# Turning the attention probabilities by 32 x 32 blocks and weighing them 512 weight columns later, with every block carried from SBUF to SBUF by the weights' queue

## The chip, the cores and the metric

The kernel runs on one core of a Trainium2 chip. The metric is device time in microseconds (us), the median of several executions; profiles come from one execution each. PE is TensorE, ACT is ScalarE, DVE is VectorE, POOL is GpSimd, SP is SyncE, which here only issues transfers.

## The reference, cut to what matters

One layer of a bidirectional encoder on 256 tokens with 2048 channels: RMS norm, one wide projection, a state-space branch and an attention branch, both projected up and merged by gates, an output projection, and an MLP of four times the width. The part that the change touches is attention (16 query heads in 4 groups, 4 key/value heads of 128):

```python
q = rms_norm(q.reshape(b, s, 16, 128), q_norm_g); k = rms_norm(k.reshape(b, s, 4, 128), k_norm_g)
q = apply_rope(q, cos, sin); k = apply_rope(k, cos, sin)
sc = jnp.einsum('blkrd,bskd->bkrls', qblk * d ** -0.5, k).astype(jnp.float32)
prob = jax.nn.softmax(sc, axis=-1).astype(v.dtype)
y_attn = jnp.einsum('bkrls,bskd->blkrd', prob, v)
...
merged = jax.nn.sigmoid(gate_a) * (y_ssm @ w_ssm_up) + jax.nn.sigmoid(gate_b) * (y_attn @ w_attn_up)
x = x + merged @ w_out
```

All is float32. The kernel splits each operand of a large product into a high part (rounded by a copy) and a low part (what is left), and multiplies high by high, high by low and low by high.

## The kernel before

The weights are read once, in windows of 2048 rows by 512 columns. A window is 8 pieces of 512 KB, and a piece of w_ssm_up, w_attn_up or w_out is 12 matmuls of 512 columns on PE (`three_passes`, L1835 to L1837). The function `walk` lists the windows, and with each one the work that is done beside it ("sides"); every engine runs through the same list, so the order of its instructions follows from it: for each piece p, first the weights' own work, then each side's function with that p, in the order of the list. For a piece, SP issues the load into one of four raw buffers (L641) once VectorE has split the piece four before it (`lo_made`); ScalarE makes the high part whi three pieces ahead of PE (L668), as soon as PE is done with the piece four before it (`used`); VectorE makes the low part wlo two pieces ahead in its list (L1108).

A **block round** turns a 256 x 512 part (tokens x channels) into channels x tokens without PE: VectorE transposes each 32 x 32 block in place (`turn_blocks`, L1146), ScalarE's queue writes all of it to DRAM (`put_blocks`, L691, 512 KB), and later reads it back with the blocks in their new places (`get_blocks`, L701, four transfers of 128 KB). There are 15 such rounds: four of z, five of rope's heads (k, then four groups of q), three of merged, three of the residual.

**Attention** runs in four windows, ssm_up 0 to 3, called the first to fourth attention window here. The side `attend` of group g has four heads h. PE makes the scores of head p at pieces p = 0 to 3 (six matmuls of 256 columns into PSUM bank S[h % 2]). VectorE takes the largest (mx, L1487) and scales it (nb, L1490); ScalarE makes the exponentials and their sums (prob, L957); VectorE multiplies by the reciprocal (rden L1494, prob L1497). Then at pieces 3 to 6 PE turns the probabilities of a head with four transposes (`turn`, L1990), ScalarE and VectorE split the turned tile (pT_hi L965, pT_lo L1502), and at pieces 4 to 7 PE weighs the values with them (`weigh`, six matmuls on pT and vg into S[:, 3]). Every second head, at pieces 5 and 7, ScalarE and VectorE take the result into the attention output (a_both, L970 and L1509; a_hi and a_lo below). Beside the first attention window, rope's last group of heads (`rope`, VectorE L1449 to L1472 with two steps on GpSimd, and a turning) and the fetch of the third (`heads_in`, L941 on ScalarE, L1481 on VectorE) are done; beside the second the fetch of the last and the first gating (`gated_a`, L1529).

## Time and profile before

| | |
|---|---|
| median of 3 runs | 1610.12 us (1608.63 to 1610.78) |
| profiled execution | 1609.39 us, span 1607.3 us |
| PE busy | 1595.4 us, 99% of the span |
| PE weight loads | 1349.2 us, 84% |
| VectorE busy | 1278.8 us, 80% |
| ScalarE busy | 928.0 us, 58% |
| transfers of the weights' queue (q1) | 302.2 MB, 58.5% of 16 engines' span |
| transfers of ScalarE's queue (q10) | 24.4 MB, 5.2% |
| granted clock of PE | 0.998 of full |

The profile is of one execution. Busy times of PE are those of pipelined matmuls: a matmul of 512 columns is shown as 0.39 us long, and the next starts 0.23 us after it. So time on PE is read from starts, not from durations. A wait is shown as the idle time before an instruction with the engine that ended it.

### The profile page before, as it was taken

Reading aid. Unit: us, or ns where it says so; the run is one execution under the profiler, and the core shown is the slowest. Engines: PE = TensorE matmul, PEld = TensorE weight load, DVE = VectorE, ACT = ScalarE, POOL = GpSimd, SP = SyncE. Lnnn points to the kernel's source line nnn. Section 1 sums busy time; section 2 is a strip of 40 time slices with the busy share of each in tenths; the row PEclk is TensorE's granted clock in tenths of the full one; section 3 lists DMA queues with packets and bytes.
Section 4 is the critical chain, followed back from the end, with each engine's and each line's share of the span. In section 5 each row is a group of like instructions: output and inputs, shape, how many; then the busy total and the mean of one; then the engine's idle time right before and its main releaser. Section 6 shows DMA issues by size and latency. Waiting matters only on the chain.

```text
span 1607.3 us, 20614 instructions
## 1 busy us (share of the span) xinstructions
PE 1595.4 (99%) x7984; PEld 1349.2 (84%) x7984; DVE 1278.8 (80%) x1521; ACT 928.0 (58%) x1264; POOL 79.2 (5%) x67
## 2 busy tenths in 40 slices
PE   9999999999999999999999999999999999999998
PEld 7888888888888888888888888888888888888886
DVE  7978877888767688876666667999899988998893
ACT  7665566665666545554445555665566655655562
POOL 3000000000000134000000000000000000000000
PEclk9999999999999999999999999999999999999999
DMA  7665656665688776545877875558645863686461
GB/s 272 202 201 184 201 183 211 197 198 185 196 244 238 231 225 200 172 145 181 244 265 235 278 228 178 181 171 266 188 133 200 275 192 123 204 281 214 143 244 53
DMA packets 144993, 327.93 MB, mean 204 GB/s; under 512 B 10944, under 2 KB 19328, under 8 KB 144768
## 3 DMA queue, kind: packets, MB, share of 16 engines
q1 hardware_dynamic: 129376, 302.21, 58.5%
q10 hardware_dynamic: 15520, 24.41, 5.2%
q8 instruction: 63, 1.03, 0.2%
q14 instruction: 34, 0.28, 0.1%
HBM read 316.55 MB, written 10.03 MB: 203 GB/s over the span
## 4 chain that ended last, share of the span: by engine, by line
PE 95%; DVE 2%; issue 1%; DMA 1%; ACT 0%; POOL 0%; POOLq 0%; SPq 0%; ACTq 0%
PE G L1835 17%; PE G L1836 17%; PE G L1837 17%; PE G L1844 13%; PE S L1844 7%; PE G L1848 6%; PE S L1835 4%; PE S L1836 4%; PE S L1837 4%; PE S L1848 4%; PE S L1962 1%; DMA raw<-in_w_in 1%; DVE wlo L1108 1%; PE S L1990 0%; PE S L1939 0%
## 5 line engine op out<-in xcount | busy, mean ns | idle before, releaser
L668 ACT ACTIVATE whi<-raw 128x1024 fp32r<-128x1024 f32 x395 | 416.6, 1059 | 396.4 <-PE G L1837 230.4
L1108 DVE TENSOR_TENSOR wlo<-raw,whi 128x1024 fp32r<-128x1024 f32 x395 | 483.3, 1238 | 132.1 <-ACT whi L668 130.5
L1835 PE MATMUL G<-whi,a_both 128*128 128x512 f32 x768 | 300.0, 391 | 2.5 <-DVE wlo L1108 2.0
L1837 PE MATMUL G<-whi,a_both 128*128 128x512 f32 x768 | 299.0, 389 | 0.0
L1836 PE MATMUL G<-wlo,a_both 128*128 128x512 f32 x768 | 299.0, 389 | 0.0
L1844 PE MATMUL G<-a_both,whi 128*128 128x512 f32 x640 | 201.5, 396 | 0.0
L1835 PEld LDWEIGHTS G<-whi,a_both 128*128 128x128 f32 x768 | 144.2, 188 | 34.0 <-issue 2.8
L1837 PEld LDWEIGHTS G<-whi,a_both 128*128 128x128 f32 x768 | 144.2, 188 | 30.2
L1836 PEld LDWEIGHTS G<-wlo,a_both 128*128 128x128 f32 x768 | 144.2, 188 | 28.9
L1848 PEld LDWEIGHTS G<-a_both,wlo 128*128 128x128 f32 x640 | 120.2, 188 | 28.3
L1835 PE MATMUL G<-whi,b_hi 128*128 128x512 f32 x342 | 133.5, 390 | 0.0
L1836 PE MATMUL G<-wlo,b_hi 128*128 128x512 f32 x342 | 133.4, 390 | 0.0
L1837 PE MATMUL G<-whi,b_lo 128*128 128x512 f32 x342 | 133.1, 389 | 0.0
L668 ACT ACTIVATE whi_late<-raw 128x1024 fp32r<-128x1024 f32 x85 | 89.0, 1058 | 66.2 <-PE S L1848 22.3
L1848 PE MATMUL G<-a_both,wlo 128*128 128x256 f32 x640 | 125.8, 278 | 0.0
L1108 DVE TENSOR_TENSOR wlo_late<-raw,whi_late 128x1024 fp32r<-128x1024 f32 x85 | 102.4, 1221 | 24.1 <-ACT whi_late L668 23.8
L668 ACT ACTIVATE whi_late<-gates 128x1024 fp32r<-128x1024 f32 x67 | 70.1, 1057 | 49.2 <-PE G L1848 18.3
L1844 PEld LDWEIGHTS G<-a_both,whi 128*128 128x128 f32 x640 | 97.5, 189 | 0.1
L1108 DVE TENSOR_TENSOR wlo_late<-gates,whi_late 128x1024 fp32r<-128x1024 f32 x67 | 81.1, 1221 | 18.5 <-ACT whi_late L668 18.5
L668 ACT ACTIVATE whi<-gates 128x1024 fp32r<-128x1024 f32 x63 | 66.1, 1055 | 38.1 <-PE G L1848 13.9
L1108 DVE TENSOR_TENSOR wlo<-gates,whi 128x1024 fp32r<-128x1024 f32 x63 | 76.4, 1221 | 12.7 <-ACT whi L668 12.1
L1844 PE MATMUL G<-a_both,whi_late 128*128 128x512 f32 x256 | 80.5, 396 | 0.0
(313 smaller groups left out, 2689.1 us busy)
## 6 DMA issues: line engine op xcount, KB each, us to landing
raw<-in_w_in SPq DMA_DIRECT2D x208, 512.0 KB, 4.4
raw<-in_w_mlp_in SPq DMA_DIRECT2D x74, 512.0 KB, 4.6
raw<-in_w_mlp_out SPq DMA_DIRECT2D x74, 512.0 KB, 4.9
gates<-in_w_mlp_in SPq DMA_DIRECT2D x54, 512.0 KB, 4.2
gates<-in_w_mlp_out SPq DMA_DIRECT2D x54, 512.0 KB, 4.8
raw<-in_w_ssm_up SPq DMA_DIRECT2D x32, 512.0 KB, 3.8
raw<-in_w_attn_up SPq DMA_DIRECT2D x32, 512.0 KB, 4.5
raw<-in_w_out SPq DMA_DIRECT2D x32, 512.0 KB, 5.2
```

The costliest lines, as they stand in the source:

```text
L668: act.activation(high(m), piece(n), ACT.Copy).then_inc(hi_made, 1)
L1108: dve.tensor_tensor(low(m), piece(n), high(m).bitcast(F32), ALU.subtract).then_inc(lo_made, 1)
L1835: pe.matmul(out_ap, hi[:, k, cols], w_hi, start=start, stop=False)
L1836: pe.matmul(out_ap, hi[:, k, cols], w_lo, start=False, stop=False)
L1837: return pe.matmul(out_ap, lo[:, k, cols], w_hi, start=False, stop=stop)
L1844: pe.matmul(banks[:, c, :], high(m)[:, cols[kk]], a_both[:, 2 * p + kk, :, :].rearrange("p h t -> p (h t)"), start=(p + kk == 0), stop=False)
L1848: last = pe.matmul(banks[:, c, 0:T], low(m)[:, cols[kk]], a_hi[:, 2 * p + kk, :], start=False, stop=(2 * p + kk == KT - 1))
L1962: last = pe.matmul(S[:, 2, (4 * c + h) * HD:(4 * c + h + 1) * HD], mw[:, 0, h, c, :], tm[:, c, h * HD:(h + 1) * HD], start=True, stop=True)
```

## The change

Three things change. First, the blocks of all rounds go from SBUF to SBUF: for each of the 16 pairs (i, j) one transfer of 32 partitions by 256 numbers, 32 KB (`block_across`). SP issues them between the loads of the weights, four after a load, seven pieces behind the load just issued (`SP_LAG`). `put_blocks`, `get_blocks` and the DRAM tensor are gone. Second, the probabilities take the same way, two heads at a time: VectorE turns their blocks (`turn_prob`, two transposes of 128x512), 16 transfers carry them, and ScalarE and VectorE split 1024 columns at once; PE's transposes and bank S[:, 2] for them are gone. Third, everything behind that moves to a new side, `weighed`, one window later: the weighing of heads 0 and 1 stands at piece 3, of heads 2 and 3 at piece 5. In the first attention window `rope` stands ahead of `attend`. A few buffers lie elsewhere. The pieces of the diff stand in the order of the kernel: constants and helpers, the order table, SP's loads, ScalarE, VectorE, PE.

```diff
-    window(13, 0, "ssm_up", 0, [("heads_in", 3), ("attend", 0), ("rope", 4)])
-    window(13, 1, "ssm_up", 1, [("heads_in", 4), ("attend", 1), ("gated_a", 0)])
-    window(14, 0, "ssm_up", 2, [("attend", 2), ("gated_a", 1)])
-    window(14, 1, "ssm_up", 3, [("attend", 3), ("gated_a", 2)])
-    window(15, 0, "attn_up", 0, [("gated_a", 3)])
+    window(13, 0, "ssm_up", 0, [("heads_in", 3), ("rope", 4), ("attend", 0)])
+    window(13, 1, "ssm_up", 1, [("weighed", 0), ("heads_in", 4), ("attend", 1), ("gated_a", 0)])
+    window(14, 0, "ssm_up", 2, [("weighed", 1), ("attend", 2), ("gated_a", 1)])
+    window(14, 1, "ssm_up", 3, [("weighed", 2), ("attend", 3), ("gated_a", 2)])
+    window(15, 0, "attn_up", 0, [("weighed", 3), ("gated_a", 3)])
...
+SP_LAG = 7
...
+        def block_across(i, j, src, dst):
+            return sp.dma_start(dst[Q * j:Q * (j + 1), i, :, :, :].rearrange("p c b t -> p (c b t)"),
+                                src[Q * i:Q * (i + 1), j, :, :, :].rearrange("p c b t -> p (c b t)"))
+
+        def across(rnd, j, src, dst):
+
+            d = BLOCK_ROUNDS.index(rnd)
+            sp.wait_ge(blocks_turned, d + 1)
+            for i in range(4):
+                block_across(i, j, src, dst).then_inc(s_across, 16)
+
+        def rope(p, n):
+            if p == 6 and n:
+                sp.wait_ge(r_lo, n)
+            if p >= 6:
+                across(("rope", n), p - 6, rope_blocks(n), last_heads if n == 4 else head_blocks)
...
+        def pair_across(g, pair, b0, b1):
+
+            sp.wait_ge(at_turned, 2 * g + pair + 1)
+            if g:
+                sp.wait_ge(at_pt_lo, 2 * g - 1 + pair)
+            elif pair:
+                sp.wait_ge(r_lo, 4)
+            for b in range(b0, b1):
+                block_across(b % 4, b // 4, prob_blocks[pair], prob_in[pair]).then_inc(at_across[pair], 16)
+
+        def attend(p, g):
+            if p in (3, 4):
+                pair_across(g, 0, 6 * (p - 3), 6 * (p - 3) + 6)
+            if p == 5:
+                pair_across(g, 0, 12, 16)
+            if p in (6, 7):
+                pair_across(g, 1, 6 * (p - 6), 6 * (p - 6) + 6)
+
+        def weighed(p, g):
+            if p == 0:
+                pair_across(g, 1, 12, 16)
...
                 sp.dma_start(dst, src).then_inc(landed[piece_slot(n)], 16)
+                if n >= SP_LAG:
+                    then, done_beside = BESIDE[n - SP_LAG]
+                    for name, at in done_beside:
+                        if name in table:
+                            table[name](then, at)
...
-            def copy_pt(h):
-                act.wait_ge(at_t, 4 * g + h + 1)
-                if 4 * g + h:
-                    act.wait_ge(at_pv, 4 * g + h)
-                act.activation(pT_hi[:, :, :].rearrange("p s l -> p (s l)"), S[:, 2, :], ACT.Copy
-                               ).then_inc(at_pt, 1)
+            if p < 4:
+                exps(p)
+
+        def weighed(p, g, pr, pp):
+            def high_pt(pair):
+                act.wait_ge(at_across[pair], 256 * (g + 1))
+                if 2 * g + pair:
+                    act.wait_ge(at_pv, 4 * g + 2 * pair)
+                act.activation(by_block(pT_hi, 0, 4), prob_wide[pair], ACT.Copy).then_inc(at_pt, 1)
...
-            if 3 <= p < 7:
-                copy_pt(p - 3)
+            if p == 1:
+                high_pt(0)
+            if p == 3:
+                high(0)
+            if p == 4:
+                high_pt(1)
             if p == 5:
-                high(0)
-            if p < 4:
-                exps(p)
-            if p == 7:
                 high(1)
...
-            def low_pt(h):
-                dve.wait_ge(at_pt, 4 * g + h + 1)
-                dve.tensor_tensor(pT_lo[:, :, :].rearrange("p s l -> p (s l)"), S[:, 2, :],
-                                  pT_hi[:, :, :].rearrange("p s l -> p (s l)").bitcast(F32), ALU.subtract
-                                  ).then_inc(at_pt_lo, 1)
+            def turn_prob(pair):
+                dve.wait_ge(at_v, (4 * g + 2 * pair + 2) * AT_V)
+                if g:
+                    dve.wait_ge(at_across[pair], 256 * g)
+                elif pair:
+                    dve.wait_ge(r_v, 5 * ROPE_V)
+                for tb in range(TB):
+                    last = dve.transpose(
+                        prob_blocks[pair][:, :, :, tb, :].rearrange("p j c t -> p c j t"),
+                        prob[:, tb, 2 * pair:2 * pair + 2, :].rearrange("p h (s j w) -> p (h s) j w", s=TB, w=Q))
+                last.then_inc(at_turned, 1)
+
+            if p < 4:
+                biggest(p)
+            if 1 <= p < 5:
+                normalise(p - 1)
+            if p == 3:
+                turn_prob(0)
+            if p == 5:
+                turn_prob(1)
+
+        def weighed(p, g, pr, pp):
+            def low_pt(pair):
+                dve.wait_ge(at_pt, 2 * g + pair + 1)
+                dve.tensor_tensor(by_block(pT_lo, 0, 4), prob_wide[pair], by_block(pT_hi, 0, 4).bitcast(F32),
+                                  ALU.subtract).then_inc(at_pt_lo, 1)
...
-            if p < 4:
-                biggest(p)
-            if 3 <= p < 7:
-                low_pt(p - 3)
-            if 1 <= p < 5:
-                normalise(p - 1)
+            if p == 1:
+                low_pt(0)
+            if p == 3:
+                low(0)
+            if p == 4:
+                low_pt(1)
             if p == 5:
-                low(0)
-            if p == 7:
                 low(1)
...
-                if h >= 2:
+                if g or h >= 2:
                     pe.wait_ge(at_exp, 8 * g + 2 * (h - 1))
...
-            def turn(h):
-                pe.wait_ge(at_v, (4 * g + h + 1) * AT_V)
-                if 4 * g + h:
-                    pe.wait_ge(at_pt_lo, 4 * g + h)
-                for sb in range(TB):
-                    for tb in range(TB):
-                        last = pe.transpose(S[:, 2, sb * T + tb * P:sb * T + (tb + 1) * P],
-                                            prob[:, h, tb, sb * P:(sb + 1) * P], ident[:, :])
-                last.then_inc(at_t, 1)
-
+            if p < 4:
+                scores(p)
+
+        def weighed(p, g, pr, pp):
             def weigh(h):
-                pe.wait_ge(at_pt_lo, 4 * g + h + 1)
+                pe.wait_ge(at_pt_lo, 2 * g + h // 2 + 1)
...
-            if 3 <= p < 7:
-                turn(p - 3)
-            if p < 4:
-                scores(p)
-            if 4 <= p < 8:
-                weigh(p - 4)
+            if p == 3:
+                weigh(0)
+                weigh(1)
+            if p == 5:
+                weigh(2)
+                weigh(3)
```

On PE, the weighing of head 2 in the first attention window, ahead of the next piece of the weights (G is the weights' product, S the attention's banks). Before:

```order
L1837 MATMUL G<-whi,b_lo 128x512
L1990 MATMUL S<-ident,prob 128x128 x4
L1835 MATMUL S<-pT_hi,vg_hi 128x256
L1836 MATMUL S<-pT_lo,vg_hi 128x256
L1837 MATMUL S<-pT_hi,vg_lo 128x256
```

After, at piece 3 of the second attention window, the first of the twelve matmuls that weigh group 0's heads 0 and 1:

```order
L1926 MATMUL G<-whi,b_lo 128x512
L1924 MATMUL S<-pT_hi,vg_hi 128x256
L1925 MATMUL S<-pT_lo,vg_hi 128x256
L1926 MATMUL S<-pT_hi,vg_lo 128x256
```

The transposes are gone, and two heads are weighed in one go.

On VectorE, pieces 3 and 4 of the second attention window (wlo is the weights' low part, mx to prob belong to the scores of group 1). Before:

```order
L1108 TENSOR_TENSOR wlo<-raw,whi 128x1024 [waits hi_made]
L1487 TENSOR_REDUCE mx<-S 128x2 [waits at_sc]
L1490 TENSOR_SCALAR nb<-mx 128x2 [waits at_max]
L1502 TENSOR_TENSOR pT_lo<-S,pT_hi 128x512 [waits at_pt]
L1494 RECIPROCAL rden<-den 128x2 [waits at_exp]
L1497 TENSOR_SCALAR prob<-prob,rden 128x256 [waits at_v]
L1497 TENSOR_SCALAR prob<-prob,rden 128x256
L1108 TENSOR_TENSOR wlo<-raw,whi 128x1024 [waits hi_made]
L1502 TENSOR_TENSOR pT_lo<-S,pT_hi 128x512 [waits at_pt]
```

After (the numbers at the buffers' ends are the compiler's):

```order
L1178 TENSOR_TENSOR wlo<-raw,whi 128x1024 [waits hi_made]
L1600 TENSOR_TENSOR a_both<-S,a_both 128x2x256 [waits at_hi]
L1557 TENSOR_REDUCE mx<-S 128x2 [waits at_sc]
L1560 TENSOR_SCALAR nb<-mx 128x2 [waits at_max]
L1564 RECIPROCAL rden<-den 128x2 [waits at_exp]
L1567 TENSOR_SCALAR prob<-prob,rden 128x256 [waits at_v]
L1567 TENSOR_SCALAR prob<-prob,rden 128x256
L1577 STREAM_TRANSPOSE prob_blocks_126<-prob 128x4x4x32 [waits at_across0,at_v]
L1577 STREAM_TRANSPOSE prob_blocks_126<-prob 128x4x4x32
L1178 TENSOR_TENSOR wlo<-raw,whi 128x1024 [waits hi_made]
L1594 TENSOR_TENSOR pT_lo<-head_blocks,pT_hi 128x1024 [waits at_pt]
```

The low part of the attention output now stands ahead of the maximum, and two transposes stand between it and the next wlo and pT_lo.

On SP, where before only the loads of w_ssm_up stood in a row, the end of the first attention window after the change (last_heads and head_blocks are the buffers that the blocks are carried to):

```order
L738 DMA raw<-in_w_ssm_up 128x2x512
L629 DMA last_heads<-q_blocks_135 32x256 x4
L629 DMA head_blocks<-prob_blocks_127 32x256 x6
L738 DMA raw<-in_w_ssm_up 128x2x512
L629 DMA last_heads<-q_blocks_135 32x256 x4
L629 DMA head_blocks<-prob_blocks_127 32x256 x6
L738 DMA raw<-in_w_ssm_up 128x2x512
L629 DMA head_blocks<-prob_blocks_127 32x256 x4
```

Up to ten block transfers stand between one load and the next.

## Rows read from the trace of the kernel before

**Rows 1.** The page, parts 1 and 4

```profile
PE 1595.4 (99%) x7984; PEld 1349.2 (84%) x7984; DVE 1278.8 (80%) x1521; ACT 928.0 (58%) x1264; POOL 79.2 (5%) x67
...
PE 95%; DVE 2%; issue 1%; DMA 1%; ACT 0%; POOL 0%; POOLq 0%; SPq 0%; ACTq 0%
```

**Rows 2.** Waits of PE, 570 to 760 us: us in total, times, longest

```profile
PE S L1835 <- DVE pT_lo L1502: 0.3, 1, 0.3
```

**Rows 3.** Busy us (instructions) of each engine by stretch, granted clock, DMA share

```profile
622.84:652.96 30.12, 29.82 (x162) 25.17 (x161) 25.04 (x44) 16.66 (x32) 7.09 (x6) 1.00 0.53 162
...
682.37:711.70 29.33, 29.33 (x162) 25.22 (x161) 20.40 (x36) 15.15 (x30) 1.14 (x2) 1.00 0.45 144
...
630.00:655.00 25.00, 24.70 (x133) 20.73 (x132) 24.29 (x43) 14.69 (x27) 8.76 (x8) 1.00 0.51 160
```

**Rows 4.** Line 1990, the transposes: ns min/median/max, first and last start

```profile
L1990 PE MATMUL S<-ident,prob x64: 270/272/301, 636.0 to 736.9; 128*128 128x128 f32 x64
```

**Rows 5.** Timeline of PE: start us, us, engine, line, operation, shapes, count

```profile
652.13 0.39 PE L1835 MATMUL S<-pT_hi,vg_hi 128*128 128x256 f32 x1 [0.30 <-DVE pT_lo L1502]
...
659.16 0.28 PE L1835 MATMUL S<-kT_hi,qT_hi 128*128 128x256 f32 x1
...
662.62 0.28 PE L1835 MATMUL S<-kT_hi,qT_hi 128*128 128x256 f32 x1
...
663.21 0.28 PE L1837 MATMUL S<-kT_hi,qT_lo 128*128 128x256 f32 x1
...
669.98 0.60 PE L1990 MATMUL S<-ident,prob 128*128 128x128 f32 x4
...
673.87 0.60 PE L1990 MATMUL S<-ident,prob 128*128 128x128 f32 x4
...
674.90 0.28 PE L1837 MATMUL S<-pT_hi,vg_lo 128*128 128x256 f32 x1
```

**Rows 6.** Timeline of VectorE in the first two attention windows

```profile
626.50 0.69 DVE L1487 TENSOR_REDUCE mx<-S 128x2 f32<-128x512 f32 x1 [2.90 <-PE S L1837]
...
639.90 1.87 DVE L1497 TENSOR_SCALAR prob<-prob,rden 128x256 f32<-128x256 f32 x2
...
650.26 1.22 DVE L1481 TENSOR_TENSOR qT_lo<-head_blocks,qT_hi 128x1024 fp32r<-128x1024 f32 x1
...
667.43 0.69 DVE L1487 TENSOR_REDUCE mx<-S 128x2 f32<-128x512 f32 x1 [1.16 <-PE S L1837]
...
668.24 0.69 DVE L1502 TENSOR_TENSOR pT_lo<-S,pT_hi 128x512 fp32r<-128x512 f32 x1
...
669.03 0.62 DVE L1497 TENSOR_SCALAR prob<-prob,rden 128x256 f32<-128x256 f32 x2
...
677.11 1.22 DVE L1108 TENSOR_TENSOR wlo<-raw,whi 128x1024 fp32r<-128x1024 f32 x1
```

**Rows 7.** Timeline of VectorE, a block turning of rope

```profile
651.99 1.29 DVE L1146 STREAM_TRANSPOSE q_blocks<-tmp_a 128x512 f32<-128x512 f32 x2
```

**Rows 8.** Timeline of ScalarE in the second attention window

```profile
668.37 0.47 ACT L957 ACTIVATE prob<-S,nb 128x256 f32<-128x256 f32 x1 [1.05 <-DVE nb L1490]
...
672.84 1.05 ACT L941 ACTIVATE qT_hi<-head_blocks 128x1024 fp32r<-128x1024 f32 x1
...
675.28 0.60 ACT L965 ACTIVATE pT_hi<-S 128x512 fp32r<-128x512 f32 x1 [1.40 <-PE S L1837]
```

**Rows 9.** Timeline of ScalarE, the last attn_up window

```profile
824.51 1.06 ACT L668 ACTIVATE whi<-raw 128x1024 fp32r<-128x1024 f32 x1 [5.84 <-DMA raw<-in_w_out]
```

**Rows 10.** Line 701, ScalarE's fetches: ns of an issue, us to landing

```profile
L701 ACTq DMA_DIRECT2D head_blocks<-block_rows x20: 309/453/1522, 541.6 to 662.5; - x20
...
DMA to landing us min/median/max: 2.6/4.8/8.8
```

**Rows 11.** Transfers in 824 to 827 us: packets, MB, share of 16 engines

```profile
q1 hardware_dynamic: 578, 1.12, 103.8%
```

**Rows 12.** The same view in 818 to 821 us

```profile
q10 hardware_dynamic: 236, 0.23, 23.0%
```

More of the change, by code:

```diff
@@ L253, in due_halves, with beside_pieces, window @@
     return blocks[:cut], blocks[cut:]
+SP_LAG = 7
+def beside_pieces():
+    beside = {}
+    def window(r, par, kind, idx, sides):
+        for p in range(PIECES):
+            beside[piece_number(r, par, p)] = (p, sides)
+    walk(None, window)
+    return beside
+BESIDE = beside_pieces()
 def previous(r, par):
@@ L346, in build @@
     v_sb = place("v_sb", [P, TB, KVH, AD])
-    prob = place("prob", [P, 4, TB, T])
+    prob = place("prob", [P, TB, 4, T])
     assert top[0] <= end_y
@@ L388, in build @@
     kT_lo = place("kT_lo", [P, KVH, T], F32R)
-    pT_hi = place("pT_hi", [P, TB, T], F32R)
-    pT_lo = place("pT_lo", [P, TB, T], F32R)
+    pT_lo = place("pT_lo", [P, 2 * TB, T], F32R)
     vg_hi = place("vg_hi", [P, TB, AD], F32R)
@@ L602, in window @@
+        def weighed(p, g):
+            if p == 0:
+                pair_across(g, 1, 12, 16)
+        table = {f.__name__: f for f in (zgate, zturned, rope, heads_in, weighed, attend, merged, residual)}
         def window(r, par, kind, idx, sides):
@@ L1063, in finish @@
                     final_squares(j, tb)
-        table = {f.__name__: f for f in (rates, decays, conv, scan, gate, zgate, zturned, rope, heads_in, values, attend, merged,
+        table = {f.__name__: f for f in (rates, decays, conv, scan, gate, zgate, zturned, rope, heads_in, values, weighed, attend, merged,
                                          residual, hidden, finish)}
@@ L2027, in residual @@
                 last.then_inc(row_mm, 1)
-        table = {f.__name__: f for f in (rates, decays, conv, scan, attend, merged, residual)}
+        table = {f.__name__: f for f in (rates, decays, conv, scan, weighed, attend, merged, residual)}
         def last_window(r, par, idx):
```

94 lines of the change are left out of this document (49 added, 45 removed).

## The prediction

> **What bounds the kernel now.** I read the page first: PE is busy 99% of the span and the chain that ended last lies 95% on PE [rows 1]. A busy PE need not be a PE at its peak, so next comes the table of PE's waits in the attention windows: one wait of 0.3 us, for VectorE's pT_lo [rows 2]. So the time is the sum of what PE is given to do, and any other engine matters only where it comes too late. Then the stretches: the first attention window takes 30.1 us and the third 29.3 us, and VectorE is busy 25.0 and 20.4 us of them, in the 25 us from 630 on even 24.3 [rows 3]. In the first window VectorE is the second bound, with little room.
>
> **The PE work that goes.** 64 transposes of prob, busy 272 ns each [rows 4], add up to 17.4 us. The steps of PE say otherwise. With four transposes in it a step (one piece, then the attention part) takes 673.87 - 669.98 = 3.89 us, without them 662.62 - 659.16 = 3.46 us, and both hold six small matmuls beside the piece [rows 5]. Four transposes cost 0.43 us, 16 such blocks 6.9 us; that is what I take. The Trainium skill, "Perfetto Trace Analysis", section Identifying the Most-Contended Engine, says that matmul busy time misleads because matmuls are pipelined; the rows agree, and by the busy time the kernel would come out 10.5 us faster than by the steps. The wait of the first window goes too, since pT_lo no longer follows at VectorE's heels: 0.4 us (weighing starts at 652.13 [rows 5], and by steps of 3.9 us it was due at 651.7). Weighing keeps its 12 small matmuls per pair of heads. Six small matmuls take 0.71 us (662.62 to 663.21 and one spacing more [rows 5]), so a bare piece takes 2.75 us. The first window becomes 8 x 2.75 + 4 x 0.71 = 24.8 us, the next three 24.8 + 4 x 0.71 = 27.7 us, and the first attn_up window gets 2.8 us of weighing. PE's own account: -6.9 - 0.4 = -7.3 us.
>
> **VectorE in the first window.** It loses four pT_lo and two a_lo there, 0.6 us each from start to next start, and gains four transposes of 128x512, 1.29 us for two [rows 7]: 3.6 us off, 2.6 us on, but PE's window shrinks by 5.3 us. Its list, by starts of the next instruction [rows 6]: 8 wlo of 1.22 less a small overlap, 9.2; 4 maxima with nb, 668.24 - 667.43 = 0.81, 3.2; 4 normalisings of 0.16 + 0.62 less overlap, 2.9; the new transposes 2.6; rope (two reduces 1.3, scale 0.1, products 1.3, two halves 2.6, turning 1.3) 6.6; heads' low part 1.2. That is 25.7 us for 24.8 us of PE, and one normalising took 1.87 us instead of 0.62 [rows 6] while GpSimd computed for rope, so about 27. What it has to spend is its lead. Whi of a piece is begun three pieces (8.2 us) before PE wants the piece and wlo ends 2.3 us later (1.06 + 1.22), a lead of 5.9 us; 2.9 us of it pass in the wait for the first scores [rows 6]. 5.9 - 2.9 - (27 - 24.8) leaves 0.8 us, against which stand the waits for GpSimd's root and for later scores. Bounds for PE's wait at the end of this window: 0, and 2.6 us. The latter so: VectorE is full from 630 on, what goes before the low part at 650.26 [rows 6] (three pT_lo, one a_lo, 2.4 us) is replaced by 2.6 us, so wlo for the next window's first piece again ends at about 650.3, but PE now wants it at 622.84 + 24.84 = 647.7. I take the middle, 1.3 us.
>
> **The chain in the next three windows.** Let the fourth piece start at 0. PE does the piece (2.75), weighing of heads 0 and 1 (4.17), scores of head 3 (4.88), the fifth piece (7.63), the sixth (10.38), and then wants pT_lo of the second pair. VectorE stands at a_lo until ScalarE has a_hi: 4.17 + 0.26 (pT_hi starts at 675.28 [rows 8], the last small matmul before it at 674.90 [rows 5], which the next follows after 0.12) + 0.6 = 5.05. Behind that wait are queued, in its order: a_lo to 5.65, maximum and nb to 6.45, normalising to 7.2, the two new transposes to 8.5, wlo to 9.65, pT_lo (1024 wide from SBUF like qT_lo, 1.22 [rows 6]) to 10.9. ScalarE meanwhile does the exps from 6.5 (two of 0.47 [rows 8]), whi and pT_hi (1.05 like qT_hi [rows 8]) to 9.5, so it is not the last. PE waits 10.9 - 10.4 = 0.5, with the hand-over 0.6 us, in each of three windows, and in the first of them 0.5 us more, because VectorE arrives late. Sum 2.3 us. Bounds: 0 (each step 0.1 us shorter is enough) and 4. The wlo queued in this chain is wanted at 13.8 at the latest and ready at 9.65. In the attn_up window that weighs the last group no scores stand between; no wait.
>
> **ScalarE and SP.** ScalarE loses 75 issues of transfers and half its copies' number; it waits for PE now, so this is worth nothing. SP gets 15 rounds of 16 block transfers and 128 for the probabilities, 368 in all, and behind each stands a weight load. Their semaphores are raised by VectorE in the step before (SP's lag of seven pieces against VectorE's lead of two), so the waits hold nothing back. What an SBUF to SBUF transfer of 32 KB costs no row shows. The densest place: from the fourth piece of the first attention window to the second of the next, with rope's last round in it, 6, 6, 4, 10, 10, 8, 4 = 48 transfers in seven steps, about 20.4 us of PE. Issue: 0.31 us at least and 0.45 at the median [rows 10]; at 0.33, 48 x 0.33 + 7 x 0.37 = 18.4 us, at 0.45 24.2 us, then 4 us late. Queue: 1.12 MB of weights took 3 us at full share, so 512 KB take 1.4 us [rows 11]; a packet of 1 KB took 23% of 16 x 3 us / 236 = 47 ns [rows 12]. A block is 32 such packets over 16 engines, 0.09 us, with a semaphore packet 0.14 us. That is the lower end; the upper is 2.6 us, the shortest landing of a 128 KB transfer [rows 10], if nothing overlapped. I take 0.14, the nearest row: 48 x 0.14 + 7 x 1.4 = 16.5 us, less than 20.4. A load may also be late: ScalarE stood 5.84 us for one [rows 9], and PE had no wait there. So 0. At that same place, where three loads of x go before the weights of out, the last round of merged now stands in line behind the weights, but the DRAM copies that shared the engines are gone: 0, bounds -0.4 and +2 us.
>
> **Sum.** -7.3 + 1.3 + 2.3 = -3.7 us on the profiled execution's 1609.4 us (span 1607.3): 1605.7. The median of the runs lies 0.7 above that execution: 1606.4 us.
>
> **Rivals.** B, the waits stay away. For it: through a longer handshake in four windows PE waited only 0.3 us [rows 2]. Against: the chain above has no idle time in it. Gain 7.3 less up to 1.5: 1603.5 to 1605.
>
> C, VectorE eats the gain: 2.6 us in the first window, 4 in the others, up to 2 at the out window; 1607.8 to 1612. For it: VectorE's 24.3 of 25 us [rows 3]. Against: its lead is rebuilt in the bare pieces of each window.
>
> D, slower: the blocks hold up the weights in their common queue. In the seven steps this decides from (20.4 + 5.8 - 9.8) / 48 = 0.34 us a block, the 5.8 being the lateness that [rows 9] shows to be free. At 0.45 us PE waits 48 x 0.45 + 9.8 - 26.2 = 5.2 us: 1611.6. At 0.6 us 12.4 us there and 32 x 0.6 + 6 x 1.4 - 26 = 1.6 us in each of three later places: 1623.6. For it: four to six transfers in line before each weight load where there were none. Against: 47 ns a packet [rows 12].
>
> The Trainium skill, "DMA: Bandwidth & Descriptors", sections Rules for kernel authors and Bandwidth, says that transfers under 64 KB pay mostly overhead, and gives 0.95 us of engine time for 64 KB; at 0.8 us a block, an estimate from that page, D's formula gives 22 + 3 x 8 = 46 us, 1652 us. No row here shows such small transfers in a line; the packet times speak for overlap.
>
> **Chances.** Forecast (1605 to 1607.8) 0.48, B 0.19, C 0.17, D 0.16, 0.04 of it beyond 1640. A measurement of this kernel can't tell less than 0.2%, 3.2 us, from no change, so faster means below 1606.9: B and 0.33 of the forecast, 0.52. The rest of the forecast and C give 0.31, D and the tail of C 0.17. The range is 1602.5 to 1614.5: about 0.02 lies below, 0.12 above. The forecast's own range is 1604.5 to 1608.
>
> **What would show it.** Right: steps of 3.46 us where 3.89 stood; PE waits for wlo at the end of the first window and once for pT_lo, 0.5 to 1.2 us, in each of the next three, 3 to 4.5 us together; VectorE full in the first window; weights that land under 8 us. Wrong: no wait for pT_lo (B); waits for wlo of over 3 us in all (C); ScalarE waiting for weights so long that PE does too, or SP issues above 0.5 us (D).

## The result, and the profile after

The changed kernel takes 1633.99 us (median of 4 runs, 1633.73 to 1635.49), the kernel before 1609.75 us beside it: a ratio of 1.0153, 95% interval 1.0135 to 1.0170. It is 24 us slower, where a gain of 3.7 us was forecast, and lies 19.5 us above the range. The profiled executions differ by their spans, 1632.3 - 1607.3 = 25.0 us, which is the number to be explained.

The page of the changed kernel, parts 1 and 4, which answer to [rows 1]:

```profile
PE 1598.4 (98%) x7920; PEld 1348.8 (83%) x7920; DVE 1287.3 (79%) x1529; ACT 927.5 (57%) x1256; POOL 77.3 (5%) x67
...
PE 81%; DVE 6%; SPq 5%; DMA 3%; ACT 2%; issue 2%; POOL 0%; POOLq 0%; DVEq 0%; ACTq 0%
```

PE is still busy 98%, but the chain that ended last is on PE for 81% only; 5% of it now are issues of SP, which had 0% before. The table of PE's waits over the whole span says more (us in total, times, longest); before there were 4.3 us of such waits in all:

```profile
PE S L1924 <- DVE pT_lo L1594: 10.9, 4, 5.4
...
PE G L1924 <- DVE wlo L1178: 8.8, 7, 4.5
...
PE S L1945 <- DVE gates L1653: 2.9, 1, 2.9
...
PE S L1945 <- DVE tmp_b L1640: 1.4, 1, 1.4
```

The waits have grown to 26.2 us, 22 us more. A wait is followed by a second loss, which the busy table of five stretches shows (us, busy us and instructions of PE, its weight loads, VectorE, ScalarE and GpSimd, then the granted clock, DMA share, GB/s); the first row is the first attention window and answers to [rows 3]:

```profile
623.03:649.84 26.81, 25.48 (x122) 20.57 (x120) 23.27 (x41) 14.01 (x27) 6.11 (x6) 1.00 0.53 161
...
660.00:680.00 20.00, 14.61 (x73) 12.62 (x73) 12.01 (x25) 8.85 (x19) 0.64 (x2) 0.84 0.47 138
...
760.00:780.00 20.00, 16.35 (x71) 13.28 (x70) 12.65 (x14) 8.85 (x9) 0.00 (x0) 0.91 0.61 195
...
840.00:860.00 20.00, 14.27 (x59) 11.55 (x60) 13.15 (x13) 10.69 (x12) 0.00 (x0) 0.91 0.71 232
...
940.00:960.00 20.00, 17.15 (x86) 14.93 (x85) 15.29 (x19) 12.43 (x19) 1.61 (x1) 0.83 0.90 332
```

In the kernel before, every 20 us slice of these parts has a granted clock of 1.00. Here the clock stood at 1.00 too until PE had stood idle for some us; then comes a stretch at the lower of its two levels, 1.2 instead of 2.4 GHz. It can begin while PE still waits: in the wait that ends at 676.21 us the clock is at the lower level from about 673.6 us on, with PE idle (0.91 over 2 us is 0.36 us at half the clock, then 0.50 throughout; the columns as above):

```profile
672.00:674.00 2.00, 0.00 (x0) 0.00 (x0) 0.00 (x0) 1.10 (x2) 0.00 (x0) 0.91 0.28 70
674.00:676.20 2.20, 0.00 (x0) 0.00 (x0) 1.27 (x2) 0.90 (x1) 0.00 (x0) 0.50 0.34 98
```

PE's timeline behind the wait at 764 us shows it; below it stand the starts of two heads' scores, one step apart:

```profile
764.29 0.38 PE L1924 MATMUL S<-pT_hi,vg_hi 128*128 128x256 f32 x1 [3.65 <-DVE pT_lo L1594]
...
765.83 0.63 PE L1924 MATMUL G<-whi,a_both 128*128 128x512 f32 x1
...
766.25 0.63 PE L1925 MATMUL G<-wlo,a_both 128*128 128x512 f32 x1
...
769.46 0.40 PE L1924 MATMUL G<-whi,a_both 128*128 128x512 f32 x1
...
769.70 0.39 PE L1925 MATMUL G<-wlo,a_both 128*128 128x512 f32 x1
```

```profile
652.66 0.28 PE L1924 MATMUL S<-kT_hi,qT_hi 128*128 128x256 f32 x1
...
656.12 0.28 PE L1924 MATMUL S<-kT_hi,qT_hi 128*128 128x256 f32 x1
```

A weights' matmul starts 0.42 us after the one before it at first and 0.24 us from 769.46 on. From one head's scores to the next it is 656.12 - 652.66 = 3.46 us, as [rows 5] had it without transposes. Between 560 and 1000 us the trace has four stretches at the lower level, 20.5 us together. In 3.5 us of them PE was idle, and these are in the waits already; in the other 17.0 us it worked at half the clock, which cost it 8.5 us. The account then is: 21.9 us more of idle time (PE is busy 439.7 us between 560 and 1000 us before and 417.8 us after), 8.5 us of clock, less 5.4 us by which PE's busy time is shorter where nothing is late and the clock is full (run e4 below): 25.0 us. By steps the transposes took 6.9 us with them. The other 1.5 us are hidden in the waits: a matmul of 512 columns is shown until 0.39 us after its start and the next was due after 0.23 us, so each wait costs PE 0.16 us more than the idle time that is shown.

By PE's timeline the difference arises in three places: 15.9 us from the first attention window to the first matmul of the first out window, with the wait before it (205.4 us of PE's time before, 221.3 after), 3.1 us from there to PE's turning of the last merged round (5.6 and 8.7 us), and 3.0 us from that to the turning of the last residual round (88.1 and 91.1 us), behind which another 2.8 us are lost at the lower clock.

**The first place, from SP to PE.** SP's timeline from the end of the first attention window on (start, us, engine, line, operation, count):

```profile
647.46 3.67 SPq L629 DMA_DIRECT2D prob_in<-prob_blocks  x6
...
664.72 3.70 SPq L629 DMA_DIRECT2D head_blocks<-prob_blocks  x6
...
668.47 0.58 SPq L738 DMA_DIRECT2D raw<-in_w_ssm_up  x1
...
671.60 2.49 SPq L629 DMA_DIRECT2D last_heads<-q_blocks  x4
```

From 642.7 to 676 us SP never stands still: six blocks take it 3.7 us, four 2.4 us, so 0.61 to 0.62 us a block, and a load behind blocks 0.58 us instead of 0.37 us. The load at 668.47 is the one that ScalarE, VectorE and PE wait for, in that order:

```profile
672.90 1.06 ACT L770 ACTIVATE whi<-raw 128x1024 fp32r<-128x1024 f32 x1 [3.08 <-DMA raw<-in_w_ssm_up]
...
673.86 1.04 ACT L1043 ACTIVATE pT_hi<-head_blocks 128x1024 fp32r<-128x1024 f32 x1
```

```profile
674.93 1.23 DVE L1594 TENSOR_TENSOR pT_lo<-head_blocks,pT_hi 128x1024 fp32r<-128x1024 f32 x1 [3.12 <-ACT pT_hi L1043]
```

```profile
676.21 0.58 PE L1924 MATMUL S<-pT_hi,vg_hi 128*128 128x256 f32 x1 [5.39 <-DVE pT_lo L1594]
```

ScalarE waits 3.08 us for the load issued at 668.47 us, and pT_hi of heads 2 and 3 stands behind that piece's whi in its queue ([rows 8] had ScalarE waiting for PE there). VectorE gets pT_hi 3.12 us late, and PE waits 5.39 us. The name in PE's table is VectorE's pT_lo, and VectorE itself waited: the last link that is late is a load. Between 640 and 780 us ScalarE waits 31.6 us for loads in all, and for none in the kernel before.

The 160 blocks of the z, merged and residual rounds by SP's line 629 (duration min/median/max in ns; the other 208 have the same median, 590 or 591):

```profile
L629 SPq DMA_DIRECT2D turned_to<-blocks x160: 507/590/1788, 443.8 to 933.0; - x160
...
DMA to landing us min/median/max: 1.8/3.0/6.3
```

And the DMA queues in the densest stretch, 642 to 677 us:

```profile
q1 hardware_dynamic: 3938, 4.98, 47.2%
```

The 16 engines are busy 47% with this queue there. It isn't full, and in the kernel before, where no load is late, it is 46.8% in the same stretch. What differs is how SP feeds it.

**The second place**, the first out window, where three loads of x stand before the weights ([rows 9, 11] in the kernel before). SP's timeline before and after:

```profile
812.13 1.53 SPq L618 DMA_DIRECT2D gates<-in_x  x3
813.71 21.61 SPq L641 DMA_DIRECT2D raw<-in_w_out  x8
```

```profile
826.34 2.41 SPq L629 DMA_DIRECT2D turned_to<-blocks  x4
...
828.79 3.23 SPq L715 DMA_DIRECT2D gates<-in_x  x3
...
832.06 0.47 SPq L738 DMA_DIRECT2D raw<-in_w_out  x1
...
832.57 3.74 SPq L629 DMA_DIRECT2D turned_to<-blocks  x4
```

```profile
841.88 1.06 ACT L770 ACTIVATE whi<-raw 128x1024 fp32r<-128x1024 f32 x1 [11.08 <-DMA raw<-in_w_out]
```

The first load of out is issued 3.3 us after the first of x (before: 1.6 us), behind four blocks, and ScalarE can start on it 9.8 us after its issue. Before, these were 824.51 - 813.71 = 10.8 us, so the load isn't longer under way; it is issued too late. PE wanted it 14.5 us after its issue before (first matmul of out at 828.23 us) and 844.34 - 4.55 - 832.06 = 7.7 us after it now. Of the 6.8 us of lead that are lost, 4.2 lie between the last load of attn_up and this one (6.2 us from issue to issue, 2.0 before), the rest was lost earlier. ScalarE waits 11.08 us for it where it waited 5.84, and what cost PE nothing then costs 4.55 us now, with 1.4 us more at the turning behind it.

### The profile page after: what moved, and what is told of

It reads as the page before. It is cut to its first block, busy times and chain, and to the rows that moved or that the text cites. A ratio compares the mean times of both kernels' runs of the same rounds, so it can differ in the third digit from the quotient of the medians.

```text
span 1632.3 us, 20789 instructions
## 1 busy us (share of the span) xinstructions
PE 1598.4 (98%) x7920; PEld 1348.8 (83%) x7920; DVE 1287.3 (79%) x1529; ACT 927.5 (57%) x1256; POOL 77.3 (5%) x67
## 3 DMA queue, kind: packets, MB, share of 16 engines
q1 hardware_dynamic: 147040, 314.29, 60.4%
## 4 chain that ended last, share of the span: by engine, by line
PE 81%; DVE 6%; SPq 5%; DMA 3%; ACT 2%; issue 2%; POOL 0%; POOLq 0%; DVEq 0%; ACTq 0%
PE G L1924 13%; PE G L1925 13%; PE G L1926 13%; PE G L1933 13%; PE S L1933 7%; PE G L1937 6%; SPq L629 4%; PE S L1937 4%; PE S L1924 3%; PE S L1925 3%; PE S L1926 3%; DVE wlo L1178 3%; DMA turned_to<-blocks 1%; PE S L2051 1%; DMA raw<-in_w_attn_up 1%
## 5 line engine op out<-in xcount | busy, mean ns | idle before, releaser
L1924 PEld LDWEIGHTS G<-whi,b_hi 128*128 128x128 f32 x342 | 64.9, 190 | 20.4 <-issue 6.3
```

The source lines that it names most:

```text
L1924: pe.matmul(out_ap, hi[:, k, cols], w_hi, start=start, stop=False)
```

## The experiments

Before is 1609.9 to 1610.7 us in every group of runs. Prices are taken from the medians; S is the theory that SP's issues cost, Q that packets and bytes in the queue do, V that VectorE does.

| run | what differs | us | ratio to before, 95% |
|---|---|---|---|
| changed kernel | | 1634.0 | 1.0135 to 1.0170 |
| e4 | no probability blocks, rounds through DRAM | 1606.2 | 0.9967 to 0.9984 |
| e3 | 128 blocks on SP, rounds through DRAM | 1614.8 | 1.0018 to 1.0039 |
| e9 | as e3, 112 of the blocks cut to 1 KB | 1609.9 | 0.9992 to 1.0010 |
| e5 | as e3, blocks spread evenly | 1622.2 | 1.0061 to 1.0086 |
| e2 | kernel before, 240 blocks of rounds on SP | 1626.3 | 1.0086 to 1.0113 |
| e1 | changed kernel, 240 blocks cut to 4 KB | 1617.2 | 1.0030 to 1.0061 |
| e8 | changed kernel, half the transfers of double size | 1611.2 | 0.9999 to 1.0017 |
| e7 | changed kernel, blocks issued by GpSimd | 1677.5 | 1.0394 to 1.0426 |
| e6, e12 | probabilities through DRAM by ScalarE | 1609.4, 1608.3 | 0.9981 to 0.9999, 0.9974 to 0.9992 |
| e10 | the same by SP | 1607.3 | 0.9976 to 0.9994 |
| e11 | as e10, transfers back one load later | 1628.1 | 1.0090 to 1.0118 |

**e4: the change without its transfers.**

```diff
-            for b in range(b0, b1):
-                block_across(b % 4, b // 4, prob_blocks[pair], prob_in[pair]).then_inc(at_across[pair], 16)
...
-                act.wait_ge(at_across[pair], 256 * (g + 1))
+                act.wait_ge(at_turned, 2 * g + pair + 1)
```

> As the run with the probabilities' blocks alone on SP, but their 128 transfers are left out: the probabilities' split reads a buffer of old numbers, all else (VectorE's turning, the wide splits, the weighing one window later) is there. This is the change without the price of its transfers; the forecast's sum for it is -3.7 us, 1606 us. Theory S: 1604 to 1607 us. Rival V: over 1615 us. The difference to the run with the 128 transfers is what these cost where SP has no other blocks: by S under 2 us.

Measured 1606.2 us (1605.0 to 1608.7), near the forecast's 1606.4; against the 1610.5 us of before beside it 4.3 us are gained. PE's busy time on the page, and three rows of PE's table of waits (1.9 us of the first lie in the first 100 us of the span, where the kernel before has 2.0):

```profile
PE 1590.0 (99%) x7920; PEld 1342.9 (84%) x7920; DVE 1288.6 (80%) x1529; ACT 927.1 (58%) x1256; POOL 77.3 (5%) x67
...
PE G L1884 <- DVE wlo L1140: 3.2, 5, 1.5
...
PE S L1905 <- DVE tmp_b L1600: 1.1, 1, 1.1
...
PE S L1884 <- DVE pT_lo L1554: 0.7, 3, 0.2
```

pT_lo costs 0.24 us in each of three windows, wlo 1.3 us at the end of the first. V is ruled out: VectorE's list, fuller by the turning, is the same as in the changed kernel, which takes 27.8 us more. That loss comes from the way of the blocks.

**e3: the probabilities' blocks alone**, with `put_blocks` and `get_blocks` of the kernel before back for the 15 rounds.

```diff
-        table = {f.__name__: f for f in (zgate, zturned, rope, heads_in, weighed, attend, merged, residual)}
+        table = {f.__name__: f for f in (weighed, attend)}
```

> The changed kernel with the 15 rounds put back on ScalarE and through DRAM; only the 128 blocks of the probabilities are issued by SP. Theory S: 32 x 0.61 + 8 x 0.58 = 24.2 us of SP in a window of 27.7 us, the densest place has 32 blocks instead of 48, so no wait for weights in the attention windows; the late places are those of the kernel before; 1603 to 1610 us, the forecast's own sum gives 1606. Rival Q (0.6 us of queue for a block): as S. Rival V: PE's waits for pT_lo of 5.4, 1.6 and 3.7 us stay, with the clock behind them, 1620 to 1626 us.

1614.8 us, outside what S gave. The 128 blocks cost 8.5 us over e4: PE waits 2.5 us at 673 us and 3.0 us at 759 us for pT_lo, with slices at 0.91 to 0.96 of the clock. The mean over a window that I had argued with (24.2 of 27.7 us) hides that the 32 blocks stand behind six of eight loads, 4.4 us of SP a step where PE takes 2.75 to 4.2. V's 1620 is not met either.

**e2: the rounds alone**, in the kernel before.

```diff
-                act.dma_start(dst[Q * j:Q * (j + 1), :, :, :, :].rearrange("w i c b t -> w i (c b t)"), rows[j]
-                              ).then_inc(s_got, 16)
+                block_across(i, j, src, dst).then_inc(s_across, 16)
```

> The kernel before, with only the 15 rounds (240 blocks) moved to SP; PE turns the probabilities as before. Theory S: no dense place in the attention windows (16 blocks in a window of 29 us, 16 x 0.61 + 8 x 0.58 = 14.4 us of SP), so no wait there; the waits of the changed kernel at the first out window (4.5 + 1.4 us) and at the first mlp_in window (2.9 us) stay with the lower clock behind them (1.8 and 3.4 us): 1609.7 + 14 = 1621 to 1626 us. Rival Q: as S. Rival V: 1608 to 1612 us, since VectorE's list is that of before.

1626.3 us, 0.3 us above S's range. Rows of PE's table of waits (1.8 us of the second lie in the span's first 100 us):

```profile
PE S L1892 <- DVE tmp_b L1587: 4.6, 1, 4.6
...
PE G L1871 <- DVE wlo L1144: 6.2, 5, 1.8
...
PE S L1892 <- DVE gates L1600: 2.6, 1, 2.6
```

All but the first window's 0.3 us lie at 813 to 844 us and at 937 us, in the merged and residual rounds; the z and rope rounds, 144 of the 240 blocks, cost nothing. Over before 15.7 us, with e3's 8.5 us over e4 24.2 us; the changed kernel is 27.8 us above e4. The 3.6 us left may be what the last rope round and the probabilities cost together, but they are no more than the intervals of the four runs leave open.

**e1: the bytes cut, the number kept.**

```diff
-            return sp.dma_start(dst[Q * j:Q * (j + 1), i, :, :, :].rearrange("p c b t -> p (c b t)"),
-                                src[Q * i:Q * (i + 1), j, :, :, :].rearrange("p c b t -> p (c b t)"))
+            return sp.dma_start(dst[Q * j:Q * j + rows, i, :, :, :].rearrange("p c b t -> p (c b t)"),
+                                src[Q * i:Q * i + rows, j, :, :, :].rearrange("p c b t -> p (c b t)"))
```

> The changed kernel with the same 368 block transfers, of which 240 (three of four rounds of z, two of three of merged, all of the residual's, and all of the probabilities' but the first pair's) carry 4 of their 32 partitions, an eighth of the packets and bytes; 28 partitions of each stay behind. Theory S (what costs is SP's time for an issue, 0.61 us from start to start, whatever a transfer carries): issues stay at 0.59 us, ScalarE's waits for weights and PE's waits stay, 1630 to 1637 us. Rival Q (packets and bytes in the weights' queue hold the weights up): most waits behind 676 us go, 1610 to 1618 us. Rival V (VectorE's fuller list is what makes PE wait): the same 1630 to 1637, with issues that may become shorter.

1617.2 us. Both theories hit one half: the issues stay as S said, and the time falls as Q said. ScalarE's waits for loads between 640 and 780 us stay too, 29.4 us for 31.6. SP's timeline and the loads' waits in the last attention windows, first e1, then the changed kernel at the same place:

```profile
747.62 0.44 SPq L739 DMA_DIRECT2D raw<-in_w_attn_up  x1
...
748.15 3.69 SPq L629 DMA_DIRECT2D head_blocks<-prob_blocks  x6
...
751.40 1.06 ACT L771 ACTIVATE whi<-raw 128x1024 fp32r<-128x1024 f32 x1 [3.17 <-DMA raw<-in_w_attn_up]
```

```profile
752.04 0.58 SPq L738 DMA_DIRECT2D raw<-in_w_attn_up  x1
...
752.72 3.68 SPq L629 DMA_DIRECT2D head_blocks<-prob_blocks  x6
...
756.27 1.06 ACT L770 ACTIVATE whi<-raw 128x1024 fp32r<-128x1024 f32 x1 [3.35 <-DMA raw<-in_w_attn_up]
```

Six issues take 3.69 and 3.68 us, 0.61 us each whether a block has 32 packets or 4. But the load behind them is issued in 0.44 instead of 0.58 us and ScalarE starts on it after 751.40 - 747.62 = 3.8 instead of 756.27 - 752.04 = 4.2 us. PE's waits at 707, 764, 844 and 944 us shrink to 0.8, 1.1, 0.5 and none (the one at 853 us grows from 1.4 to 2.3), and no slice behind 680 us has a lower clock any more. The wait in the dense place (4.27 instead of 5.39 us) stays; 32 of the 48 blocks there were left whole, so this run doesn't tell what their bytes cost.

**e9: the same for the probabilities alone.**

```diff
-                block_across(b % 4, b // 4, prob_blocks[pair], prob_in[pair]).then_inc(at_across[pair], 16)
+                block_across(b % 4, b // 4, prob_blocks[pair], prob_in[pair], 1 if g or pair else Q).then_inc(at_across[pair], 16)
```

> e3_probs_alone (128 blocks on SP, rounds through DRAM, 1614.8 us) with 112 of the 128 blocks cut to one partition, 1 KB, the rest of each left behind. The price of the 128 full blocks is e3 less e4_no_prob_blocks, 1614.8 - 1606.2 = 8.5 us. Theory S (issues): 1613 to 1615 us. Rival Q (packets): 1606 to 1608 us. Both: between, and e1 makes me expect about half, 1610 us.

1609.9 us: of e3's price of 8.5 us, 3.7 us stay with next to no bytes (the intervals leave about 2 us either way). But for the 16 whole blocks they are issues. ScalarE's waits for loads between 640 and 780 us stay as well, 17.8 us for e3's 18.3. A load behind six of the 1 KB blocks still takes 0.58 us to issue, so what went here didn't go by a shorter issue of the loads.

**e8: the number halved, the bytes kept.** A packet carries 2 KB instead of 1 KB here, so the blocks' packets are halved with the issues (138,208 packets in the queue over the whole run, 147,040 in the changed kernel).

```diff
-            return sp.dma_start(dst[Q * j:Q * (j + 1), i, :, :, :].rearrange("p c b t -> p (c b t)"),
-                                src[Q * i:Q * (i + 1), j, :, :, :].rearrange("p c b t -> p (c b t)"))
+            return sp.dma_start(dst[Q * j:Q * (j + 1), i:i + 2, :, :, :].rearrange("p a c b t -> p (a c b t)"),
+                                src[Q * i:Q * (i + 1), j - j % 2:j - j % 2 + 2, :, :, :].rearrange("p a c b t -> p (a c b t)"))
...
-            for i in range(4):
+            for i in (0, 2):
...
-            for b in range(b0, b1):
+            for b in range(b0, b1, 2):
```

> The changed kernel with half as many block transfers (184), each of 32 partitions by 512 numbers, 64 KB, so that all bytes are moved but not each block to its place. Behind a load stand 3, 3, 2 transfers instead of 6, 6, 4, and 2 instead of 4 for a round. e1_short_blocks cut the bytes to an eighth and kept the number: 1617.2 us, with the issues still 0.61 us apart. Theory S (number of issues): the waits go, 1606 to 1611 us. Rival Q (bytes): 1628 to 1634 us as the changed kernel. If both have their part, as e1 speaks for, 1612 to 1624 us.

1611.2 us, just above S's range and below the one for both: 22.8 of 27.8 us are gone. The double blocks take the same issue (SP's line 629, the 80 of z, merged and residual):

```profile
L629 SPq DMA_DIRECT2D turned_to<-blocks x80: 507/588/1514, 443.6 to 908.7; - x80
```

And the queue in 642 to 677 us:

```profile
q1 hardware_dynamic: 4142, 7.19, 71.3%
```

The median issue is 588 ns for 64 KB as it was 590 for 32 KB, and the queue's share in 642 to 677 us, where it was 47.2%, has risen to 71%: it carries more and PE waits less (0.24 us at each pT_lo). The bytes alone are thus not what costs; whether it is the number of issues or that of packets this run can't tell, and e1 and e9, which cut the packets alone, say that both have a part. What is left is a wait of 3.27 us at 833 us, in the out window, with a lower clock behind it (0.83 in the slice from 820 us).

**e5: the same 128 blocks spread evenly.**

```diff
-            if p in (3, 4):
-                pair_across(g, 0, 6 * (p - 3), 6 * (p - 3) + 6)
-            if p == 5:
-                pair_across(g, 0, 12, 16)
-            if p in (6, 7):
-                pair_across(g, 1, 6 * (p - 6), 6 * (p - 6) + 6)
+            if 3 <= p < 7:
+                pair_across(g, 0, 4 * (p - 3), 4 * (p - 3) + 4)
+            if p == 7:
+                pair_across(g, 1, 0, 4)
```

The other 12 of the second pair stand behind the next window's first three loads.

> As e3_probs_alone, but the probabilities' 128 blocks stand four behind each load in all eight pieces instead of 6, 6, 4, 6, 6, 4 behind six of them and none behind two. Bytes, packets and their number are the same. In e3 a load with six blocks behind it took SP 4.4 us for PE's 2.75 to 4.2 us, and PE waited 2.5 and 3.0 us for pT_lo. Theory S (SP's 0.62 us an issue, where the blocks stand dense): a step is 4 x 0.62 + 0.6 = 3.1 us, under PE's mean of 3.46 us, so the waits of 2.5 and 3.0 us go and the time falls from 1614.8 to 1606 to 1609 us. Rival Q (each block costs the weights' queue its time, however they are spread): 1612 to 1616 us as e3.

1622.2 us, and both missed. Who waited for the blocks, from the view of their line, first here, then in e3:

```profile
  ACT pT_hi L1027: 16.0, 8
```

```profile
  ACT pT_hi L1029: 0.8, 1
```

Between 640 and 780 us ScalarE waits 4.3 us for loads (18.3 us in e3) and 16.0 us for blocks (0.8 us there). So the loads do come in time when the blocks stand four and four, as S said of them, but the blocks themselves come late, which neither theory had, and the time doesn't decide between the two. The last four blocks of a pair stand behind one or two loads more than in e3, and SP may issue a load only when VectorE has freed its slot. A block on this queue is late by what stands before it, as a load is.

**e7: GpSimd issues all blocks.**

```diff
-            return sp.dma_start(dst[Q * j:Q * (j + 1), i, :, :, :].rearrange("p c b t -> p (c b t)"),
+            return pool.dma_start(dst[Q * j:Q * (j + 1), i, :, :, :].rearrange("p c b t -> p (c b t)"),
```

> The changed kernel, all 368 blocks from SBUF to SBUF as in it, but issued by GpSimd, which is busy 5% of the span; its copies of v stand at the window's last piece instead of the first. Theory S: SP issues loads alone as in the kernel before, so the waits for weights go and with them the lower clock; what is left is the forecast's sum, 1604 to 1610 us, if GpSimd's own issues take under about 0.7 us (32 in a window of 27.7 us, 48 in the densest 20.4 us would need 0.42 us). Rival Q (the bytes and packets cost, not the issuing): 1620 to 1634 us. Open from both: if a GpSimd issue takes over 1 us, the probabilities' blocks themselves come late and PE waits for pT_lo, 1615 us or more, with weights on time.

1677.5 us. An issue takes 0.50 us, and GpSimd stands 124.5 us, in 34 pieces, for nothing that the profile shows, between groups of two to ten blocks:

```profile
L1754 POOL DMA_DIRECT2D turned_to<-blocks x160: 498/498/697, 441.6 to 976.6; - x160
...
  issue: 124.5, 34
```

The blocks come late: ScalarE waits 18.6 us for the probabilities' blocks and 34.1 us for those of z, merged and residual. Between 640 and 780 us it waits 6.2 us for loads, 31.6 in the changed kernel, with the same bytes on the same 16 engines, which speaks for S; but the kernel is slower there for other reasons and wants its loads later, so this doesn't show it. Moving the issues off SP is not enough where the other issuer stands still between them.

**e6, e12 and e10: 40 transfers instead of 128**, one to DRAM and four back for two heads, issued by ScalarE (e6, and again e12) or by SP (e10).

```diff
+            act.dma_start(prob_rows[2 * g + pair], prob_blocks[pair][:, :, :, :, :].rearrange("p j c b t -> p (j c b t)")
+                          ).then_inc(at_put[pair], 16)
...
+            for j in range(4):
+                act.dma_start(prob_in[pair][Q * j:Q * (j + 1), :, :, :, :].rearrange("w i c b t -> w i (c b t)"), rows[j]
+                              ).then_inc(at_across[pair], 16)
```

> As e3_probs_alone, but the blocks of the probabilities take the road of the other rounds: ScalarE issues one transfer to DRAM and four back for a pair of heads, 40 transfers instead of 128 and none on SP. Theory S: no block stands before a load of the weights, so the time is that of e4_no_prob_blocks plus what 40 issues cost ScalarE, which waits for PE: 1605 to 1608 us. A rival L (the way through DRAM, put and get one after the other, lands too late for the split at pieces 1 and 4): PE waits for pT_lo, over 1610 us.

> e6_probs_through_dram once more beside e11, on the same chip: ScalarE issues the 40 transfers. It gave 1609.4 us, 0.9990 of before with an interval to 0.9999. If ScalarE's issues cost what the interval leaves open, it is again 1 to 3 us above e11; if e6 only met a bad chip, both are at 1605 to 1607 us.

> e6_probs_through_dram with its 40 transfers of the probabilities issued by SP between the loads instead of by ScalarE: 5 issues for a pair where e3 has 16. By S 10 issues a window at 0.6 us are 6 us of SP's 27.7 and no load comes late: 1605 to 1609 us. If SP's wait for the landing of a put (about 4 us in e6) stands in front of loads, PE waits for wlo: over 1611 us.

1609.4, 1608.3 and 1607.3 us, where before was 1609.9, 1610.7 and 1610.0: all three intervals lie below 1. They beat the kernel before by 0.1 to 0.2%, which is a little, and the changed kernel by over 24 us. e10 has the lowest median of the versions that keep the whole computation and e12 the lowest ratio; whether ScalarE or SP issues is not told apart by intervals that overlap. e6 lies 1.4 us above S's range (1605 to 1608), e10 within it. What e12 was to be set against, e11, failed for another reason, so e12 is only a second measurement of e6. SP's issues of the transfers back in e10:

```profile
L644 SPq DMA_DIRECT2D prob_in<-prob_rows x16: 412/432/467, 649.8 to 735.2; - x16
...
DMA to landing us min/median/max: 2.7/4.4/7.0
```

**e11: the transfers back one load later.**

```diff
-            if p == 5:
-                get_prob(g, 0)
             if p == 6:
                 put_prob(g, 1)
+                get_prob(g, 0)
...
-            if p == 0:
+            if p == 1:
                 get_prob(g, 1)
```

> e10_dram_by_sp with each transfer back issued one load later (first pair of heads at piece 6, second at piece 1 of the next window), so that SP no longer stands waiting for the landing of a transfer to DRAM (6.3 us at the median) before it may issue the next load. In e10 PE waited 1.2 us for pT_lo in the second attention window and 0.6 us for wlo at the first out window. If SP's wait for that landing made these, they go: 1605 to 1607 us. If they come from what the ring of the weights' slots lets SP do, the time stays at 1607 us; if the blocks now land too late for the split, PE waits for pT_lo, 1609 us or more.

1628.1 us. ScalarE now waits for the blocks:

```profile
ACT pT_hi L1032 <- DMA prob_in<-prob_rows: 17.5, 4, 6.1
```

The third of the expected cases came, the blocks too late for the split. One load later is one slot of the ring later, and that costs far more than e10's wait of 1.2 us. e5 and e11 fail in the same way.

## Why the prediction was wrong, point by point

- **PE's work (-7.3 us): right.** Steps of 3.46 us stand where 3.89 stood. PE's busy time fell by only 5.4 us in e4, since each wait hides 0.16 us of what left; by the steps of e4, 6.9 us of transposes and the one wait are gone, as forecast.
- **VectorE in the first window (1.3 us): right by the waits shown.** 0.25 + 0.17 + 0.92 us of waits for wlo (642.7, 645.9, 649.8 us), the same within 0.04 us in e4. By its length the window lost 26.8 - 24.8 = 2.0 us, still within the bounds 0 and 2.6. VectorE is busy 23.3 of the window's 26.8 us.
- **The chain for pT_lo (2.3 us): right in place, too large.** 0.24 us in each of three windows in e4, 0.7 us in all, near rival B's zero (0.4 us each, 1.2 in all, with what the idle time hides). The forecast's sum came out all the same (1606.4 and 1606.2 us): by luck, since 1.1 us were lost at 831 us, which it had at 0. B's own times are 0.7 us too high: a gain of 7.3 less up to 1.5 on 1610.1 us is 1602.8 to 1604.3, not 1603.5 to 1605.
- **ScalarE and SP (0 us): the step that failed**, with "at 0.33, 48 x 0.33 + 7 x 0.37 = 18.4 us" and "I take 0.14". The issue of a block was priced near the lower end of issues of another kind. [Rows 10] gave 0.31 and 0.45 us for ScalarE's issues, four in a row with DRAM on one side (in e6 such a row is 0.31, 0.46 and 1.04 us for the last two, so it slows already). Here, from SBUF to SBUF, they start 0.61 us apart, above both values that the sum was tried with. With it the same sum is 48 x 0.61 + 7 x 0.58 = 33 us, where PE takes 20.4 and the lateness held to be free was 5.8. In place of "So 0" the blocks' way cost 27.8 us (e4 against the changed kernel).
- **Rival D: the right mechanism at 0.16.** "The blocks hold up the weights in their common queue", deciding from 0.34 us a block. Its case for 0.6 us gave 1623.6 and its sum for the dense place 12.4 us of waits, where 5.4 us came. Three terms were missing or too small: the clock (8.5 us), the out window (bounded at +2, it cost 7.1 us of waits), and the residual round (2.9 us), which the forecast didn't speak of. What D called the queue is two things: the issues on SP, of which e9 shows a price, and the packets before a load, of which e1 and e9 show one (e8 halves both). They don't add up to a split of the 27.8 us: halving the number takes 22.8 of them and cutting the bytes 16.8, perhaps because either makes most steps short enough again.
- **"The free 5.8 us".** ScalarE's wait at 824 us in the kernel before was taken as lateness that costs nothing. It was free there. At the same place of the changed kernel ScalarE waited 11.08 us and PE 4.55.
- **The clock** was in no term. Around the waits of 2.9 to 5.4 us of the changed kernel PE lost 1.7 to 3.0 us each by working at the lower clock, around those of 2.5 and 3.0 us in e3 1.7 and 1.5 us; the changed kernel's waits of 1.2 to 1.6 us had no lower clock with them.
- The page "DMA: Bandwidth & Descriptors" of the Trainium skill, Rules for kernel authors, says that below 64 KB one pays mostly overhead and that small transfers are to be coalesced. e8 agrees: 64 KB instead of 32 KB halves the number and takes 22.8 us off. The estimate of 0.8 us a block from its figures was too high (0.61 us measured, 1634 us instead of 1652), but nearer than the 0.14 us that I took.

What stays open: why issues in a row keep 0.61 us on SP whatever they carry, how the 27.8 us divide between issues and packets, and how much of e1's gain comes from the shorter issue of a load (0.14 us) and how much from its earlier landing (0.4 us). In e9 the load's issue stayed at 0.58 us and 4.8 us were gained all the same; for the rounds the run that would part the two was not made.

## What to carry to other kernels

Price a transfer first by its issue on the engine that issues it, and take that price from issues of the same kind in a row: here those from DRAM to SBUF start 0.46 to 0.49 us apart on SP and those from SBUF to SBUF 0.61. Then lay number times price over the steps of the bound engine, step by step at the densest place, and not over a window's mean. Where one engine issues in one row these transfers and the loads that the bound engine lives on, few large transfers through DRAM beat many small ones that go straight, here by 5.4 to 7.5 us (e6, e12 and e10 against e3). A wait of several us on a busy PE is paid again in clock, here 8.5 us with 21.9 us of waits.

## What the runs showed of the hardware

- Transfers from SBUF to SBUF issued in a row by SP start 0.61 to 0.62 us apart with 1 KB, 4 KB and 32 KB, and 0.59 us apart with 64 KB. Issues of transfers from DRAM to SBUF, four in a row, are 0.43 us long at the median on SP (e10), a load of 512 KB alone 0.33 to 0.37 us, and behind blocks of 32 KB or 1 KB 0.58 us, behind blocks of 4 KB 0.44 us.
- GpSimd issues the same blocks in 0.50 us each, but stood in 34 places between groups of two to ten, 124.5 us in all (e7).
- The clock can fall to its lower level while PE is still waiting: in the changed kernel 2.6 us before the wait at 676.21 us ended.
- The weights' queue kept the 16 DMA engines busy 47.2% in the stretch where loads were late and 46.8% in the same stretch of the kernel before, where none was: the share didn't show that the loads came late.
